# Queries of a hybrid encoder layer transposed before their norm, which moves into the softmax

## The reference

```
z = rms_norm(x) @ w_in                 # split into a, gate (convolution), q, k, v
u = a * sigmoid(gate); u = causal depthwise conv (31 taps) + bias
u = silu(layer_norm(u))
q = rms_norm(q per head of 64) * qn_g  # 16 query heads
k = rms_norm(k per head of 64) * kn_g  # 2 key heads
scores = q . k / 8 - slope[head] * |distance|   # banded: chunk of 64 and the one before
p = softmax([scores, sink[head]]) without the sink's column
x = x + concat(u, p . v) @ w_out
```

## Time and profile before

| | us |
|---|---|
| three runs | 2075.19, 2078.07, 2078.84 (median 2078.07) |
| profiled execution | 2079.59 |
| its span, first to last instruction | 2077.8 |
| TensorE busy | 2058.1 (99%) |
| VectorE, ScalarE, GpSimd busy | 1462.8, 1112.1, 472.9 |
| mean granted TensorE clock | 0.998 of full |

### The profile page before, as it was taken

The page is one execution under the profiler, slowest core; times in us unless marked ns, Lnnn a source line. Parts: engine busy times, 40 slices in busy tenths (PEclk is TensorE's granted clock), DMA queues, the critical chain, the costliest instruction groups (busy, mean ns, idle before and its releaser), DMA issues.

```text
span 2077.8 us, 24351 instructions
## 1 busy us (share of the span) xinstructions
PE 2058.1 (99%) x9598; PEld 1717.3 (83%) x9598; DVE 1462.8 (70%) x1468; ACT 1112.1 (54%) x1265; POOL 472.9 (23%) x260
## 2 busy tenths in 40 slices
PE   9989999999999999999999999999999999999999
PEld 8889788888888888888888888888888888888887
DVE  5787879946887268874776884588738983489832
ACT  6678656544555445554554554555545554455542
POOL 3676630031001410014111014400140003300033
PEclk9999999999999999999999999999999999999999
DMA  7543365555664556545566455565465555655554
GB/s 254 169 126 112 132 218 178 194 191 203 215 230 143 193 202 227 209 156 178 203 213 215 151 194 190 181 223 211 158 239 175 189 185 192 233 182 182 194 191 161
DMA packets 208450, 394.30 MB, mean 190 GB/s; under 512 B 11344, under 2 KB 21968, under 8 KB 208336
## 3 DMA queue, kind: packets, MB, share of 16 engines
q1 hardware_dynamic: 207760, 392.21, 55.5%
q10 hardware_dynamic: 576, 0.53, 0.1%
HBM read 390.60 MB, written 2.10 MB: 189 GB/s over the span
## 4 chain that ended last, share of the span: by engine, by line
PE 94%; DVE 3%; ACT 1%; DMA 1%; issue 1%; SPq 0%; DVEq 0%; ACTq 0%
PE pair L730 12%; PE pair L732 12%; PE pair L731 12%; PE pair L811 11%; PE pair L813 11%; PE pair L812 11%; PE pair L796 6%; PE pair L798 6%; PE pair L797 6%; PE tbank L826 2%; PE pair L750 1%; PE pair L752 1%; PE pair L751 1%; DVE w_lo L1707 1%; PE pair L940 1%
## 5 line engine op out<-in xcount | busy, mean ns | idle before, releaser
L1228 ACT ACTIVATE w_hi<-w_raw 128x1024 fp32r<-128x1024 f32 x584 | 615.3, 1059 | 603.1 <-PE pair L732 293.4
L1707 DVE TENSOR_TENSOR w_lo<-w_raw,w_hi 128x1024 fp32r<-128x1024 f32 x425 | 540.1, 1273 | 368.2 <-ACT w_hi L1228 368.0
L633 POOL TENSOR_TENSOR w_lo<-w_raw,w_hi 128x1024 fp32r<-128x1024 f32 x159 | 390.1, 2454 | 1569.9 <-ACT w_hi L1228 1569.9
L811 PE MATMUL pair<-w_hi,xT_hi 128*128 128x512 f32 x1040 | 404.7, 389 | 0.4 <-DVE w_lo L1707 0.4
L813 PE MATMUL pair<-w_hi,xT_lo 128*128 128x512 f32 x1040 | 404.8, 389 | 0.0
L812 PE MATMUL pair<-w_lo,xT_hi 128*128 128x512 f32 x1040 | 404.6, 389 | 0.0
L1228 ACT ACTIVATE w_hi<-s_raw 128x1536 fp32r<-128x1536 f32 x182 | 270.9, 1488 | 183.7 <-PE pair L813 124.7
L1707 DVE TENSOR_TENSOR w_lo<-s_raw,w_hi 128x1536 fp32r<-128x1536 f32 x182 | 318.2, 1759 | 63.3 <-ACT w_hi L1228 63.1
L730 PE MATMUL pair<-w_hi,yT_hi 128*128 128x512 f32 x704 | 274.8, 390 | 0.0
L732 PE MATMUL pair<-w_hi,yT_lo 128*128 128x512 f32 x704 | 274.1, 389 | 0.0
L731 PE MATMUL pair<-w_lo,yT_hi 128*128 128x512 f32 x704 | 273.8, 389 | 0.0
(11 more groups left out here) (198 smaller groups left out, 2556.8 us busy)
## 6 DMA issues: line engine op xcount, KB each, us to landing
w_raw<-in_w_down SPq DMA_DIRECT2D x176, 512.0 KB, 4.1
w_raw<-in_w_up SPq DMA_DIRECT2D x110, 512.0 KB, 6.5
w_raw<-in_w_gate SPq DMA_DIRECT2D x110, 512.0 KB, 3.8
w_raw<-in_sc_in SPq DMA_DIRECT2D x72, 512.0 KB, 4.4
s_raw<-in_w_gate SPq DMA_DIRECT2D x44, 768.0 KB, 8.4
s_raw<-in_w_up SPq DMA_DIRECT2D x44, 768.0 KB, 7.9
w_raw<-in_w_in SPq DMA_DIRECT2D x52, 512.0 KB, 4.3
w_raw<-in_w_out SPq DMA_DIRECT2D x32, 512.0 KB, 4.2
```

The costliest lines, as they stand in the source:

```text
L633: nc.gpsimd.tensor_tensor(w_lo[at], raw(o), w_hi[at].bitcast(F32), ALU.subtract).then_inc(w_lo_pool, 1)
L811: nc.tensor.matmul(b, x_hi(k, t), w_hi[:, r + kk, :], start=(first[t] and kk == 0), stop=False)
L1228: nc.scalar.activation(w_hi[:, tiles_of(o), :], raw(o), ACT.Copy).then_inc(w_hi_ready, 1)
L1707: nc.vector.tensor_tensor(w_lo[at], raw(o), w_hi[at].bitcast(F32), ALU.subtract).then_inc(w_lo_dve, 1)
```

## The change

The queries are transposed as they come from the projection, without their norm r. Since softmax needs r(q.k) - slope x distance, the kernel forms s = q.k - (slope / r) x distance and lets r enter afterwards: 1/r is made as mean square times r, then multiplied by the negative slopes, which now come from memory as a small table (`slopes`, one more load on ScalarE's queue); the row's maximum is multiplied by r before it meets the sink; the exponential takes r as its scale. The two multiplications of the queries in each group go. TensorE's transposes now wait for the copy of the queries out of PSUM (`read_out`) and not for VectorE. All four hand-written orders are written anew, with the same slots and taps in other places; on TensorE one step of the third group's probabilities stands two slots earlier.

```diff
@@ buffers
-            sb("early_end", [P, 24], F32, early)
+            slopes = sb("slopes", [P, HQ], F32, early)
+            sb("early_end", [P, 8], F32, early)
@@ TensorE
             def query_transposes(g):
-                pe.wait_ge(qk_normed, 2 + g)
+                read_out(f"q{g}")
@@
-            late(10, 14)
+            late(10, 12)
             prob_transposes(2, 0, 2)
-            late(14, 16)
+            late(12, 16)
@@ ScalarE
+            act.dma_start(slopes[:, :], tables_in[:, 2 * P + SEQ:2 * P + SEQ + HQ]).then_inc(tables_loaded, 16)
@@
-                    nc.scalar.activation(s, s, ACT.Exp, bias=neg_top[:, t, j:j + 1], accum_out=den[:, t, j:j + 1])
+                    nc.scalar.activation(s, s, ACT.Exp, bias=neg_top[:, t, j:j + 1],
+                                         scale=qk_r[1 + hh // 2][:, t, j:j + 1], accum_out=den[:, t, j:j + 1])
@@ VectorE
             def query_norms(g):
+
                 inverse_roots(1 + g)
-                for t in range(TT):
-                    q3 = heads_of(q_tok[:, t, g * NB:(g + 1) * NB])
-                    ins = nc.vector.tensor_tensor(q3, q3, qk_r[1 + g][:, t, :].unsqueeze(2).to_broadcast([P, GQ, HD]),
-                                                  ALU.mult)
-                ins.then_inc(qk_normed, 1)
+                ms, r, slope_root = (x[1 + g][:, :, :] for x in (qk_ms, qk_r, qk_t))
+                if g == 0:
+                    dve.wait_ge(tables_loaded, 32)
+                link(nc.vector.tensor_tensor(slope_root, ms, r, ALU.mult))
+                link(nc.vector.tensor_tensor(slope_root, slope_root,
+                                             slopes[:, g * GQ:(g + 1) * GQ].unsqueeze(1).to_broadcast([P, TT, GQ]),
+                                             ALU.mult))
@@
-                        slope = 2.0 ** (-8.0 * (g * GQ + j + 1) / HQ)
-                        ins = nc.vector.scalar_tensor_tensor(scores[t][:, j, 0:keys], dist[t], -slope,
+                        ins = nc.vector.scalar_tensor_tensor(scores[t][:, j, 0:keys], dist[t],
+                                                             qk_t[1 + g][:, t, j:j + 1],
                                                              tbank[b][:, m * SEQ:m * SEQ + keys], ALU.mult, ALU.add)
@@
                 link(nc.vector.reduce_max(top[:, t, :], scores[t][:, :, 0:keys], AX_X))
+                link(nc.vector.tensor_tensor(top[:, t, :], top[:, t, :], qk_r[1 + g][:, t, :], ALU.mult))
@@ the order on GpSimd, two of its lines
-            add_taps(16, 27)
+            add_taps(17, 28)
             low(35)
-            add_taps(27, 30)
+            add_taps(28, 29)
...
```

More of the change, by code:

```diff
@@ L1437, in ln_swish @@
                                      ACT.Copy).then_inc(hi_ready, 1)
-            highs(q00 + 1, q00 + 4)
-            tap_products(0, 4)
+            highs(q00 + 1, q00 + 3)
+            tap_products(0, 1)
+            highs(q00 + 3, q00 + 4)
+            tap_products(1, 4)
             read_narrow("kv", ACT.Copy, kv_tok)
@@ L1490, in _ @@
+            tap_products(52, 58)
+            highs(z0 + 12, z0 + 13)
+            tap_products(58, 61)
             highs(z0 + 13, z0 + 14)
-            tap_products(53, 58)
             heads_highs(0)
-            tap_products(58, 62)
+            highs(z0 + 14, z0 + 15)
+            tap_products(61, 62)
             u1_copy(0)
             exps(2)
-            highs(z0 + 14, z0 + 15)
-            tap_products(62, 63)
+            tap_products(62, 64)
             highs(z0 + 15, ao0)
             exps(3)
-            tap_products(63, 64)
@@ L1501, in _ @@
-            highs(ao0, ao0 + 1)
-            tap_products(64, 67)
+            highs(ao0, ao0 + 2)
+            tap_products(64, 66)
             prob_copies(2, 0, 2)
-            tap_products(67, 68)
-            highs(ao0 + 1, ao0 + 2)
-            tap_products(68, 69)
+            tap_products(66, 68)
             highs(ao0 + 2, ao0 + 3)
             gate_read(1)
-            tap_products(69, 72)
             highs(ao0 + 3, ao0 + 4)
-            tap_products(72, 73)
+            tap_products(68, 72)
@@ L1525, in _ @@
-            tap_products(82, 85)
-            highs(ao0 + 9, ao0 + 13)
-            tap_products(85, 89)
-            highs(ao0 + 13, ao0 + 16)
-            tap_products(89, 94)
-            highs(ao0 + 16, ao0 + 17)
-            tap_products(94, 100)
+            tap_products(79, 81)
+            highs(ao0 + 6, ao0 + 9)
+            tap_products(81, 83)
+            highs(ao0 + 9, ao0 + 10)
+            tap_products(83, 84)
+            highs(ao0 + 10, ao0 + 13)
+            tap_products(84, 94)
@@ L1532, in _ @@
+            highs(ao0 + 13, ao0 + 15)
+            tap_products(94, 96)
+            highs(ao0 + 15, ao0 + 17)
+            tap_products(96, 100)
             ln_table()
             ln_squares()
-            highs(ao0 + 17, ao0 + 20)
+            highs(ao0 + 17, ao0 + 19)
             ln_root()
@@ L1538, in _ @@
             ln_swish(2)
+            highs(ao0 + 19, ao0 + 20)
             ln_swish(3)
@@ L2412, in _tables @@
         parts.append(np.where(seen, np.abs(q - k), far))
+    parts.append(np.broadcast_to(-2.0 ** (-8.0 * np.arange(1, 17) / 16), (128, 16)))
     return np.concatenate(parts, axis=1).astype(np.float32)
```

181 lines of the change are left out of this document (89 added, 92 removed).

## The result

| | kernel before | changed kernel |
|---|---|---|
| median of 9 runs each, us | 2078.43 (2075.19 to 2079.93) | 2081.82 (2080.75 to 2084.49) |
| profiled execution, us | 2079.59 | 2080.95 |
| its span, us | 2077.8 | 2079.1 |

The changed kernel takes 1.0019 of the time before, 95% interval 1.0011 to 1.0028: 3.4 us more by the medians, a little under the 0.2% by which the prediction counted slower, though 1, no change, lies outside the interval. The forecast was 2075.8, the range ended at 2080.3. The two profiled executions differ by 1.4 us only (1.3 in their spans), so the profile must explain a kernel that gained nothing, and something else the rest.

What follows compares the result with a forecast made beforehand. TensorE bounds the kernel, busy 2058.1 of 2077.8 us. Of 6.7 us gained, 1.6, 2.2 and 0.6 come back, so 2.3 are saved: median 2078.07 becomes 2075.8, range 2071.5 to 2080.3.

Steps and rivals of the forecast that it cites:

- Part 1: At the query transposes: TensorE's 3.8 us wait for `q_tok` and the lower clock behind it go, 6.7 us gained.
- Part 2: At the first scores: VectorE takes them out 5.1 us earlier (range 5.1 to 7.4), giving back 1.6 of 6.7.
- Part 3: Behind score group 0's maximum: fourth small step and new neighbours cost 2.2 us; TensorE waits 2.9, clock kept.
- Part 4: Rest of the mixer: score group 2's extra small step costs 0.6 us; the other items taken as 0.
- (a): Rival: gain stays whole, small steps meet adds alone, 4.2 to 5.8 us saved, taken as 2073.0; chance 0.29.
- (b): Rival: part 3's wait reaches 3.8 us and the clock falls, 2079.6, or 2081.4 with group 2; chance 0.15.
- (c): Rival: VectorE is the bound, its saving goes into locked small steps, nothing won, 2078; chance 0.08.

Runs made afterwards that it cites:

- b_math: Kernel before with the change's arithmetic alone, its four old written orders kept: 2078.71 us, 1.0001 of the kernel before.
- a_pool: Changed kernel with only GpSimd's order altered, so adds and no low part lie beside score group 2's small steps: 2076.02 us, 0.9991 of the kernel before.
- b_clash: Kernel before with GpSimd's low part of slot 49 seven adds earlier, beside score group 2's small steps: 2082.33 us, 1.0019 of the kernel before.
- a_again: Changed kernel without any edit, timed and profiled once more: 2082.23 us, 1.0020 of the kernel before.
- b_warm: Kernel before with 16 dummy matmuls in TensorE's wait of 3.8 us for the normed queries: 2076.84 us, 0.9994 of the kernel before.
- a_fill46: Changed kernel with two k-tiles of TensorE's narrow job moved from behind the scores to ahead of the transposes that waited for `oT_lo`: 2084.01 us, 1.0026 of before.
- a_warm: Changed kernel with 20 dummy matmuls where TensorE waited 4.5 us for `oT_lo`: 2080.30 us, 1.0011 of the kernel before.
- a_lows_first: Changed kernel with VectorE's two low parts for `oT_lo` moved ahead of score group 2's small steps: 2078.45 us, 1.0001 of the kernel before.

## Why the prediction was wrong

**Part 1, the wait removed: right, and 1.6 us too small.** `q_tok` is gone from the list and the clock full at the transposes. In addition the wait of 1.8 us for `k_twice` went, which the prediction expected to come later: the transposes of the keys started 1.6 us earlier, at 82.69. The same mechanism was at work there, to the good: VectorE's last six steps for the keys took 2.67 and 4.16 us before, beside low parts and adds of GpSimd, and 0.49 and 0.90 now, with GpSimd nearly idle. "Only the first belongs to what the change removes" holds for the arithmetic (in b_math the wait for `k_twice` is still 1.8 us), not for the rewritten orders.

**Part 2, the first scores taken out 5.1 us earlier: right in kind, too small.** They came at 106.65, 8.5 us earlier (115.15 before). The root stood at 98.19, not between 100 and 102, because the loads of the highs ahead of it were there, and the five taps and four highs that follow it up to the copy of the transposes took 5.9 us, as reckoned; so the copy stood at 104.10 and not between 106 and 108. The three steps of the Newton chain and the two new ones ran with GpSimd idle, 0.17 us each. The prediction took the end that follows from a late load; the range of 5.1 to 7.4 did not reach what happened.

**Part 3, the small steps of score group 0: the mechanism right, the price of the steps too high.** They met an add, an add, one low part (2.32 us, slot 35) and an add: 4.2 us with gaps, where the three old ones had taken 3.8. Their price was 0.4, not 2.2; TensorE's wait was 1.25 and not 2.9. From the first scores taken out to the second half of score group 1 it is 10.7 us now and was 9.8: the other 0.5 are the slower scores, which part 4 put at nothing. The lead behind it was 7.6 us, and at 159 us still 7.3.

**Part 4: the step that failed.** It is the price of the fourth small step in score group 2: "Group 2's lies ahead of `oT_lo` on which TensorE waited, so 0.17 to 2.4, and I take 0.6, that beside adds." It took the old neighbours for the new: the earlier trace rows and the order rows of GpSimd were read for slots 35 and 37 only, not for slots 47 and 49, where the rewritten order puts two low parts back to back. Two of the four steps sat out a low part each, so the upper bound of 2.4 was too low as well: it counted the added step alone and not the old ones that the new order brings beside a low part. Measured: 4.2 us of waiting (4.53 against 0.35), 3.7 through the half clock behind it and 0.6 for the late low part, 8.5 where 0.6 stood. With the lead of 7.3 this is the whole result of the profile, 1.2 us lost.

The same part held that the slope from a column costs 0 and the exponential's scale up to 0.2 for a group. By the groups of instructions, one of the scores on 128 columns takes 343 ns and not 281, and an exponential 480 and not 388; 32 of each, those on 256 columns with them, make 2.0 and about 3 us on VectorE and ScalarE. The bounds were wrong, but it did not decide the result: only 0.5 us of it reached TensorE in part 3, and a_pool, with all of it, is below before.

**The clock.** The prediction made a rule of two cases: 2.3 us of wait safe, 3.8 not. The runs have no such rule. In b_clash TensorE waited 3.1 us for `q_tok` and the clock of the stretch behind stayed full; in b_math it fell to 0.50 behind 2.5 us; in a_again it fell behind waits of 0.8 and 0.3 us. It also differs between executions of one kernel, and the 2.9 us of part 1's clock, read from one profile, are not confirmed by the medians (b_warm: 1.4, not clear of the noise). A wait should have been given a chance of the fall, with the price as its size, and not a threshold.

**The rivals.** (a), the whole gain, 2073.0: a_pool, the changed kernel without the meeting, is 2.7 us below before by the medians and 5.1 by the profiled executions (2074.53, the fastest of its eleven, against 2079.59), so between the forecast and (a). That its median of 2076.0 lies on the forecast of 2075.8 is luck: parts 2 and 3 were off by 3.4 and 1.8 us, and it has a wait of 1.4 us that was not forecast. (b), slower: its mechanism is what happened (small steps beside low parts, a wait over 3.5 us, the clock behind it), but at the second place that it named only as an addition, and by two low parts. That its far end, 2081.4, lies near the 2081.8 measured is chance: its first wait did not come. Its chance of 0.15 was too small for a mechanism that could strike at any of four score groups, of which one was looked at. (c) is partly seen in a_fill46 and a_warm, where VectorE's late low part takes half of what is gained.

The rule that the prediction drew from the Trainium skill (SBUF — State Buffer, section "SBUF: two separate sides"), that VectorE with two inputs in SBUF and GpSimd exclude each other for whole instructions, holds in every trace here, with the end of each held step within 0.04 us of the end of a GpSimd instruction. The passage does not tell how many instructions in a row a step can sit out, which was three in a_lows_first and more in a_warm. Read with GpSimd's new order beside all four score groups, the rule would have shown the two low parts beside group 2, 4.5 us where 0.6 was taken.

## What to carry to other kernels

A small VectorE step on SBUF costs what GpSimd is doing beside it: count the steps, and look up in the new order of GpSimd which instruction lies beside each at every meeting with the bounding engine, not only at the place that the change is about. Where a dependent chain of n such steps hangs on a path, keep long GpSimd instructions away from it, or shorten the chain; here the place of a few adds was worth 6.2 us and a fused step 2.8. A wait moved on one engine alone comes back at the next meeting as long as the late engine stays as late (a_fill46, a_lows_first), and on a kernel at 99% of TensorE, waits and half-clock time summed over the list account for the difference between two versions to within 1 or 2 us.

## What the runs showed of the hardware

- One VectorE instruction on 8 columns can sit out more than one GpSimd instruction: 4.89 us in a_lows_first beside two low parts of 2.3 us, and 6.11 us in a_warm beside adds and two low parts, where it takes 0.17 alone (at 125.14 us in the changed kernel). In the changed kernel the same two low parts held one step each.
- Single-source steps are held as well: `neg_top<-top`, with one input in SBUF and a constant, took 2.28 and 2.32 us beside low parts.
- Beside adds the steps alternate with them at 0.66 us each.
- A column in place of a constant as scalar operand costs about 0.06 us a VectorE instruction at 128 and at 256 columns (343 against 281 ns, 474 against 413) and a column as scale about 0.09 us an exponential (480 against 388 ns, 592 against 499).
- The fall of TensorE's clock behind a wait is not fixed by the kernel: behind the same waits, of 0.8 and 0.3 us and of 2.5 us, it was there in one execution and not in the other (17.0 and 10.2 us of half clock in two profiles of the changed kernel). The eleven runs of a_again spread by 4.0 us, and the longest have the lowest mean clock.
